# In a decoder kernel, the gathered key row's product reads h from PSUM, and a sample pair's scores pass through two PSUM banks

## The chip, the cores and the metric

The kernel runs on one core of a Trainium2 chip. The metric is the device time of one execution in microseconds (us); the time before is 2462.84 us, the median of three runs (2455.85 to 2471.47).

## What is computed

One step of a one-layer hybrid decoder for 528 prompt rows (512 tokens and 16 meta tokens) and 8 x 8 sample rows with a paged past of 2048 positions each. All data is float32. Three parts of the reference matter here. `peer` is the retrieval of single-neuron experts; `fox_sample` and `dsa_sample` are the two attentions of the sample rows over the past.

```python
def peer(x, ...):                       # x is h, the normalised rows
    ...                                 # 8 heads x top-16 experts for each token
    pre = jnp.einsum('thkd,td->thk', expert_u[experts], xb)      # key rows times h
    coef = (gate * jax.nn.gelu(pre, approximate=False)).astype(x.dtype)
    return jnp.einsum('thk,thkd->td', coef, expert_v[experts])   # value rows

def fox_sample(q, k, v, logf, cache_k, cache_v, cache_logf, page_table):
    ...
    p = jax.nn.softmax(jnp.concatenate([s_past, s_new], axis=-1), axis=-1)   # 2048 + 8 keys
    ...
```

## The kernel before

The kernel has three phases: the projection, the prompt's attention, and from about 440 us a third one in which five engines follow one written plan. The plan is a list of items; each engine goes through it in the same order and does its own part of every item. Its backbone is `gathers`: 1152 indirect DMAs issued by POOL (GpSimd, L918), each of 128 expert rows of 1024 floats (512 KB). 576 of them fetch key rows (`peer_u`, v = 0) and 576 value rows (`peer_v`, v = 1). They are for five token tiles i (four of 128 prompt tokens, one of 64 sample rows, whose experts are packed so that it needs only 64 key gathers). The order is: the 128 key gathers of tile 0, 72 value gathers of tile 0, and then the key gathers of the next tile woven with value gathers of earlier ones. The rows land in a ring of 10 slots (16 late in the phase); POOL waits for a slot's last reader before it issues into it.

- A key row is read by VectorE (`read_row`, L2081): row x h, summed over 1024 elements into one column of `pre`. h is `hrow[i]` (for the last tile `h_twice`), in SBUF as the row is. The operation is a custom one followed by the reading of its accumulator.
- A value row is read by TensorE (`add_rows`, L1369): four matmuls of 512 columns for one row, summed in PSUM banks 6 and 7. Its weights are strips written by ScalarE (L1699) from the coefficients, after GELU (L1596, `gelu`) and the product with the gate (L2053, `coefs`, VectorE).
- Between the gathers lie the other items: the merge and query products of tiles 1 to 3 (L1164, L1178, L1202), the routing (top-16 and selection on VectorE, `route`), and the sample's part.

The sample's part goes through eight pairs q (0 to 3 FoX, 4 to 7 DSA). For each q, TensorE makes the scores in five pieces c (`sample_scores`: four of 512 keys in banks 0 to 3, one of 8 in bank 4), VectorE takes the maximum over 2056 (`sample_max`, L1981), ScalarE the exponential from PSUM into `prob_s` in SBUF (`exponentials`, L1635) and the normalised weights in place (L1640); TensorE turns them in 16 transposes through banks 0 to 3 (`sample_turn`, L1302), ScalarE copies them out (L1648), and TensorE multiplies them with the values (`sample_weigh`, L1325), in bank 5. Before the pairs, the index scores use banks 0 to 3 by two and two (`index_products`, L1236, `index_relu`, L1604). SyncE (SP) issues the loads of weights and pages (`k_b`, `v_b`, `kv_a`, `kidx`) in an order of its own.

Which banks a stage holds sets what can be kept in PSUM:

```python
            at = gather_at[i, 0, 0]                     # first key gather of tile i
            out = bank(c)                               # scores of piece c, banks 0 to 3
            act.activation(prob_s, ps[:, 0:KEYS], ACT.Exp, bias=col(COL_SMAX), ...)
            dve.tensor_tensor_reduce(out=row, in0=row, in1=h, ..., accum_out=pre[:, k:k + 1])
```

## Time and profile before

| what | value |
|---|---|
| median of three runs | 2462.84 us (2455.85 to 2471.47) |
| span of the profiled execution | 2493.9 us |
| busy: PE, VectorE, POOL, ScalarE | 1810.2, 1433.9, 1307.8, 307.8 us |
| moved by DMA | 791.92 MB, of it 604.58 MB by POOL's queue |

The span of the profiled execution is 1.3% above the median of the timed runs; sums are made against the span and then scaled. PE is TensorE, DVE is VectorE, ACT is ScalarE, POOL is GpSimd, SP is SyncE. Busy time is summed over the whole span and says little about which engine ends a stage; the DMA columns of a table by stretches do: the share is the mean over 16 DMA engines of the time that their packets took, and can be slightly over 1 because packets overlap.

### The profile page before, as it was taken

The numbers are of one execution on the slowest core, as the hardware profiler recorded it, in microseconds if no ns is written. First come the engines' busy times: TensorE is split into PE (matmuls) and PEld (weight loads), VectorE is DVE, ScalarE is ACT, GpSimd is POOL, SyncE is SP. The second block draws the span as 40 slices with busy tenths as digits, with TensorE's granted clock in tenths as the row PEclk, the third lists the DMA queues.
The fourth block names the chain that finished last, engine by engine and source line by source line (L and its number), as shares of the span: only waits on it lengthen the run. The fifth ranks groups of instructions, "written<-read, shape, count | busy, mean of one in ns | idle before, by whom it ended". The sixth has DMA issues, their size and how long they took to land.

```text
span 2493.9 us, 23573 instructions
## 1 busy us (share of the span) xinstructions
PE 1810.2 (73%) x7244; PEld 768.0 (31%) x7247; DVE 1433.9 (57%) x3191; ACT 307.8 (12%) x732; POOL 1307.8 (52%) x1175
## 2 busy tenths in 40 slices
PE   9999988899699635566666766776777884555566
PEld 6767646644244201111112121221223250110011
DVE  2115876898845643999856569854444437434400
ACT  0214442111011101001101010110110010000000
POOL 1100000467655744555555557766777747677664
PEclk9998987999899867777778789998999997876678
DMA  5206322999989976999999999999999999999997
GB/s 182 71 3 195 102 85 68 355 328 410 361 306 368 346 281 238 394 367 400 386 401 380 401 371 362 371 356 368 378 384 409 409 370 374 364 359 380 355 377 287
DMA packets 259648, 791.92 MB, mean 318 GB/s; under 512 B 31522, under 2 KB 56163, under 8 KB 258947
## 3 DMA queue, kind: packets, MB, share of 16 engines
q0 software_dynamic: 166400, 604.58, 63.6%
q1 hardware_dynamic: 91268, 180.82, 20.6%
q10 hardware_dynamic: 1856, 5.03, 0.5%
q8 instruction: 58, 0.95, 0.2%
q14 instruction: 66, 0.54, 0.1%
HBM read 784.13 MB, written 5.59 MB: 317 GB/s over the span
## 4 chain that ended last, share of the span: by engine, by line
POOL 13%; DMA 10%; PE 8%; issue 7%; SPq 7%; another core or an unknown queue 6%; DVE 2%; ACT 1%; POOLq 0%
POOL arena L918 13%; DMA arena<-v_b 4%; PE ps L1369 3%; SPq L841 3%; DMA arena<-peer_v,arena 3%; SPq L768 2%; DMA arena<-peer_u,arena 2%; PE ps L1325 2%; DMA arena<-kv_a 2%; SPq L834 1%; PE ps L1202 1%; DVE arena L2081 1%; PE ps L1302 1%; ACT arena L1640 0%
## 5 line engine op out<-in xcount | busy, mean ns | idle before, releaser
L1369 PE MATMUL ps<-arena 128*32 128x512 f32 x2304 | 767.5, 717 | 346.6 <-DMA arena<-peer_v,arena 287.9
L2081 DVE CUSTOM_DVE_ANT_0 arena<-arena 128x1024 f32<-128x1024 f32 x576 | 694.7, 1225 | 531.5 <-DMA arena<-peer_u,arena 475.7
L918 POOL DMA_INDIRECT arena<-peer_v,arena x576 | 623.4, 1082 | 445.9 <-PE ps L1369 245.0
L918 POOL DMA_INDIRECT arena<-peer_u,arena x576 | 664.1, 1153 | 311.8 <-issue 162.2
L1369 PEld LDWEIGHTS ps<-arena 128*32 128x32 f32 x2304 | 153.4, 122 | 877.7 <-issue 662.1
L1164 PE MATMUL ps<-arena 128*128 128x448 f32 (+2 forms) x512 | 156.8, 467 | 13.1 <-DVE arena L1997 12.4
L1202 PE MATMUL ps<-arena 128*128 128x384 f32 (+2 forms) x704 | 146.5, 368 | 10.0 <-ACT arena L1576 8.1
L1325 PE MATMUL ps<-arena 128*64 128x512 f32 (+1 forms) x512 | 102.6, 538 | 68.1 <-DMA arena<-v_b 57.3
L900 POOL MEMSET arena<- 128x1024 f32 x1 | 1.0, 953 | 282.4 <-ACTq L723 282.4
L950 PE MATMUL ps<-arena 128*128 128x296 f32 (+1 forms) x512 | 132.1, 419 | 6.2 <-DMA arena<-xT 6.2
L1699 ACT ACTIVATE arena<-arena 128x8 f32<-128x8 f32 x72 | 15.3, 216 | 943.1 <-PE ps L1369 635.2
L1202 PEld LDWEIGHTS ps<-arena 128*128 128x128 f32 x704 | 104.3, 202 | 58.9 <-issue 26.8
L1164 PEld LDWEIGHTS ps<-arena 128*128 128x128 f32 x512 | 89.0, 193 | 87.0 <-issue 70.4
L950 PEld LDWEIGHTS ps<-arena 128*128 128x128 f32 (+1 forms) x512 | 96.9, 190 | 39.7 <-issue 8.3
L1284 PE MATMUL ps<-arena 128*32 128x512 f32 x256 | 51.6, 901 | 61.3 <-DMA arena<-k_b 61.0
L1325 PEld LDWEIGHTS ps<-arena 128*64 128x64 f32 x512 | 39.7, 159 | 144.0 <-issue 143.2
L895 POOL DMA_INDIRECT arena<-logf_b,arena x16 | 14.6, 913 | 126.4 <-PE ps L950 113.6
L2088 DVE SCALAR_TENSOR_TENSOR arena<-arena,ps 128x1024 f32<-128x1024 f32 (+1 forms) x5 | 6.1, 1219 | 126.2 <-PE ps L1369 84.6
L1967 DVE MAX8 arena<-arena 64x8 f32<-64x2056 f32 x32 | 73.6, 2299 | 1.0
L979 PE MATMUL ps<-arena 64*128 64x384 f32 (+9 forms) x168 | 69.9, 525 | 4.9 <-ACT arena L1545 1.9
L1968 DVE MATCH_REPLACE8 arena<-arena 64x2056 f32<-64x2056 f32 x32 | 73.1, 2286 | 0.0
L1825 DVE MAX8 arena<-arena 128x8 f32<-128x128 f32 (+3 forms) x120 | 34.2, 325 | 58.6 <-ACT arena L1583 53.2
(211 smaller groups left out, 1694.1 us busy)
## 6 DMA issues: line engine op xcount, KB each, us to landing
arena<-k_b SPq DMA_DIRECT2D x128, 256.0 KB
arena<-v_b SPq DMA_DIRECT2D x128, 256.0 KB
arena<-w_mix SPq DMA_DIRECT2D x56, 512.0 KB
arena<-w_q SPq DMA_DIRECT2D x48, 512.0 KB
arena<-kv_a SPq DMA_DIRECT2D x128, 128.0 KB
arena<-w_out SPq DMA_DIRECT2D x24, 512.0 KB
arena<-peer_u,arena POOLq DMA_INDIRECT x576
arena<-peer_v,arena POOLq DMA_INDIRECT x576
```

Of the source, the lines that this page charges most:

```text
L841: sp.dma_start(ring[s_][:, j * 256:(j + 1) * 256], io["kv_a"][bass.ds(nos[j], 1)].rearrange("o p n -> (o p) n")).then_inc(ring_loaded[s_], 16)
L918: pool.indirect_dma_start(out=rows[slot_of[n]], out_offset=None, in_=io["peer_v"] if v else io["peer_u"], in_offset=bass.IndirectOffsetOnA ...
L950: last = pe.matmul(bank(2 * (m % 2) + a, HT, 0, n), wring[m % 3][:, k, 0:n], xT[:, k, a * HT:(a + 1) * HT], start=(k == 0), stop=(k == KD ...
L979: last = pe.matmul(out, heads[0:rows_, q, q0:q0 + nq], heads[0:rows_, kt, c0:c1], start=True, stop=not biased)
L1164: last = pe.matmul(out, mw_k[u % NMW][:, k0 + k, :], src[:, k, :], start=(k == 0), stop=(k == nk - 1))
L1202: last = pe.matmul(bank(4 + n % 2, WIDTH[p]), mw_k[u % NMW][:, k, :], hT[p][:, k, :], start=(k == 0), stop=(k == KD - 1))
L1284: last = pe.matmul(out[32 * lane:32 * lane + 32], qs_flat[:, at + 32 * lane:at + 32 * lane + 32], kk[e][:, :, hp, :], start=(hp % 2 == 0), ...
L1325: last = pe.matmul(out[e], probT_s[:, c, j * 128 + 64 * e:j * 128 + 64 * e + 64], rhs, start=(c == 0 and j == 0), stop=False)
L1369: last = pe.matmul(bank(6 + a, 512, 32 * lane, 32 * lane + 32), strips[:, GT * (G % 2) + k % GT, MID - r_:MID - r_ + 32], rows[slot_of[n]] ...
L1967: step(dve.max(top8, isamp))
L1968: step(dve.match_replace(isamp, top8, isamp, TAKEN))
L2081: dve.tensor_tensor_reduce(out=row, in0=row, in1=h, scale=1.0, scalar=0.0, op0=ALU.mult, op1=ALU.add, accum_out=pre[:, k:k + 1]).then_inc( ...
```

## The change

- `read_row` reads h from PSUM. ScalarE copies h of tile i there once, before the tile's first key row (`place_h`, a new item `h_up`): tile 0 to banks 6 and 7, the others to banks 2 and 3. VectorE waits for the copy at the first key row of each tile; the copy waits until the key rows of the tile before have been read.
- To free banks 2 and 3 from the first key row of tile 1 on, the sample's part keeps to banks 0, 1, 4 and 5. The scores of a pair go alternately to banks 0 and 1, and a new item `s_keep` has ScalarE copy each piece into `prob_s`; the maximum and the exponential then read `prob_s`. The transposes alternate between banks 0 and 1, as do the key scores of tile 4 (`score_bank`); the index products have one pair of banks instead of two.
- The plan's positions don't move: each `s_score` with its `s_keep` takes the room that `s_score` had.

The diff, without the declaration of two semaphores and the two new branches of ScalarE's loop:

```diff
@@ -171,6 +171,10 @@
+        def h_bank(i):
+            return bank(2 if i else 6, D)
...
@@ -518,7 +523,8 @@
             out += [(("iy", 4), 2), (("admit",), 1)]
-            out += [(("s_score", 0, c), 5) for c in range(5)]
+            for c in range(5):
+                out += [(("s_score", 0, c), 1), (("s_keep", 0, c), 4)]
...
@@ -526,19 +532,22 @@
                     for c in range(5):
-                        out += [(("s_score", q + 1, c), 5), (("s_weigh", q, c), 5)]
+                        out += [(("s_score", q + 1, c), 1), (("s_keep", q + 1, c), 4), (("s_weigh", q, c), 5)]
                 else:
                     out += [(("s_weigh", q, c), g if c < 4 else 1) for c in range(5)]
                     out += [(("s_out", q), 36 if q == 3 else 16)]
                     if q + 1 < NB:
-                        out += [(("s_score", q + 1, c), 3) for c in range(5)]
+                        for c in range(5):
+                            out += [(("s_score", q + 1, c), 1), (("s_keep", q + 1, c), 2)]
                 if q + 1 < NB:
                     out += [(("s_max", q + 1), 2)] + ([(("s_out", q), 1)] if q < 3 else [])
                     out += [(("s_exp", q + 1), 2), (("s_norm", q + 1), 2), (("s_turn", q + 1), 3)]
             return out
+        for i in range(1, 5):
+            put(gather_at[i, 0, 0], "h_up", i)
         in_prompt = [("turn", 0), ("score", 0, 0)] + [("query", 0, m) for m in range(4)]
-        pre_items = [("routed0",)] + [item for item, _ in merge_items(0) if item not in in_prompt]
+        pre_items = [("h_up", 0), ("routed0",)] + [item for item, _ in merge_items(0) if item not in in_prompt]
...
@@ -563,6 +572,7 @@
         s_end = at
+        assert where["score", 3, 3] < where["h_up", 1]
...
@@ -642,7 +652,7 @@
             if kind == "s_score" and at[1] == 4:
-                return sx_done, at[0] + 1
+                return s_kept, 5 * at[0] + 5
...
@@ -708,6 +718,10 @@
             return qp_ready, 2 * PH * p + m + 1
+        def score_bank(i, g):
+            return g if i < 4 else g % 2
...
@@ -1208,11 +1222,13 @@
                 pe.wait_ge(qp_copied, 2 * PH * p + 4 * g + 4)
-                if i:
+                if p == 2 and g >= 2:
+                    pe.wait_ge(sc_copied, 4 * i + g - 1)
+                elif i:
                     pe.wait_ge(sc_copied, 4 * (i - 1) + g + 1)
-                for m in range(4 * g, 4 * g + 4):
-                    last = pe.matmul(ps[0:nt, m * 128:(m + 1) * 128], qpT[p][:, m, 128 * t:128 * t + nt], subk[:, m, :],
-                                     start=True, stop=True)
+                for m in range(4):
+                    last = pe.matmul(bank(score_bank(i, g), 512, 0, nt)[:, m * 128:(m + 1) * 128],
+                                     qpT[p][:, 4 * g + m, 128 * t:128 * t + nt], subk[:, 4 * g + m, :], start=True, stop=True)
...
@@ -1227,13 +1243,13 @@
                     pe.wait_ge(qp_copied, 4 * PH)
-                if c >= 2:
-                    pe.wait_ge(ix_read, 2 * (c - 1))
+                if c:
+                    pe.wait_ge(ix_read, 2 * c)
                 w = 512 if c < 4 else SN
                 keys = unit("ki", -1, c, 0).rearrange("p (a n) -> p a n", a=4) if c < 4 else kin
                 for g in range(2):
                     for p in (2 * g, 2 * g + 1):
-                        last = pe.matmul(bank(2 * (c % 2) + g, w), qis[:, p, :], keys[:, p, :], start=(p % 2 == 0),
+                        last = pe.matmul(bank(g, w), qis[:, p, :], keys[:, p, :], start=(p % 2 == 0),
...
@@ -1258,8 +1274,10 @@
                         pe.wait_ge(smask_ready, 1)
-                if q:
-                    pe.wait_ge(st_copied, 5 * (q - 1) + c + 1)
+                if q and c in (0, 1, 4):
+                    pe.wait_ge(st_copied, 5 * (q - 1) + (3, 4, 0, 0, 5)[c])
+                if c in (2, 3):
+                    pe.wait_ge(s_kept, 5 * q + c - 1)
...
@@ -1276,7 +1294,7 @@
                     return
-                out = bank(c)
+                out = bank(c % 2)
...
@@ -1291,15 +1309,17 @@
                                   start=True, stop=False)
-                pe.matmul(out, pick[:, pr, :], bias[:, c * 512:(c + 1) * 512], start=False, stop=True)
+                pe.matmul(out, pick[:, pr, :], bias[:, c * 512:(c + 1) * 512], start=False, stop=True).then_inc(ss_ready, 1)
             def sample_turn(q):
                 pe.wait_ge(sw_ready, q + 1)
                 for c in range(5):
                     if c < 4:
+                        if c >= 2:
+                            pe.wait_ge(st_copied, 5 * q + c - 1)
                         for j in range(4):
                             k0 = c * 512 + j * 128
-                            last = pe.transpose(ps[:, k0:k0 + 128], prob_s[:, k0:k0 + 128], ident)
+                            last = pe.transpose(bank(c % 2)[:, j * 128:(j + 1) * 128], prob_s[:, k0:k0 + 128], ident)
...
@@ -1580,7 +1600,7 @@
                     act.wait_ge(pair_routed, 4 * (i - 3) + 4)
-                act.activation(sc[SCB[i]][0:nt, 4 * g:4 * g + 4, :].rearrange("p a b -> p (a b)"), bank(g, 512, 0, nt),
+                act.activation(sc[SCB[i]][0:nt, 4 * g:4 * g + 4, :].rearrange("p a b -> p (a b)"), bank(score_bank(i, g), 512, 0, nt),
...
@@ -1601,7 +1621,7 @@
                         act.wait_ge(iy_ready, c)
-                    act.activation(relu_s[g][:, 0:w], bank(2 * (c % 2) + g, w), ACT.Relu).then_inc(ix_read, 1)
+                    act.activation(relu_s[g][:, 0:w], bank(g, w), ACT.Relu).then_inc(ix_read, 1)
...
@@ -1613,7 +1633,7 @@
                 else:
-                    act.wait_ge(ss_ready, q)
+                    act.wait_ge(ss_ready, 5 * q)
...
@@ -1628,11 +1648,26 @@
+            def place_h(i):
+                act.wait_ge(ln1_done, i + 1)
+                if i:
+                    act.wait_ge(dve_used, read_before[gather_at[i, 0, 0]])
+                if i == 4:
+                    act.wait_ge(h_packed, 16 * 2)
+                act.activation(h_bank(i), hrow[i] if i < 4 else h_twice, ACT.Copy).then_inc(h_placed, 1)
+            def keep_scores(q, c):
+                act.wait_ge(ss_ready, 5 * q + c + 1)
+                if q and c == 0:
+                    act.wait_ge(st_ready, 5 * q)
+                w = 512 if c < 4 else SN
+                act.activation(prob_s[:, c * 512:c * 512 + w], bank(c % 2 if c < 4 else 4, w), ACT.Copy).then_inc(s_kept, 1)
             def exponentials(q):
                 act.wait_ge(smax_ready, q + 1)
-                if q:
-                    act.wait_ge(st_ready, 5 * q)
-                act.activation(prob_s, ps[:, 0:KEYS], ACT.Exp, bias=col(COL_SMAX),
+                act.activation(prob_s, prob_s, ACT.Exp, bias=col(COL_SMAX),
...
@@ -1644,7 +1679,7 @@
                     act.wait_ge(st_ready, 5 * q + c + 1)
-                    dst, src = (probT_s[:, c, :], bank(c)) if c < 4 else (probTn, bank(4, 128, 0, SN))
+                    dst, src = (probT_s[:, c, :], bank(c % 2)) if c < 4 else (probTn, bank(4, 128, 0, SN))
...
@@ -1975,10 +2014,10 @@
             def sample_max(q):
-                dve.wait_ge(ss_ready, q + 1)
+                dve.wait_ge(s_kept, 5 * q + 5)
                 if q:
                     dve.wait_ge(sx_done, q)
-                dve.tensor_reduce(col(COL_SMAX), ps[:, 0:KEYS], AX_X, ALU.max, negate=True).then_inc(smax_ready, 1)
+                dve.tensor_reduce(col(COL_SMAX), prob_s, AX_X, ALU.max, negate=True).then_inc(smax_ready, 1)
...
@@ -2074,11 +2113,10 @@
                 row = rows[slot_of[n]]
-                h = hrow[i] if i < 4 else h_twice
-                if i == 4 and k == 0:
-                    dve.wait_ge(h_packed, 16 * 2)
+                if k == 0:
+                    dve.wait_ge(h_placed, i + 1)
                 dve.wait_ge(row_loaded[slot_of[n]], 16 * fill_of[n])
-                dve.tensor_tensor_reduce(out=row, in0=row, in1=h, scale=1.0, scalar=0.0, op0=ALU.mult, op1=ALU.add,
+                dve.tensor_tensor_reduce(out=row, in0=row, in1=h_bank(i), scale=1.0, scalar=0.0, op0=ALU.mult, op1=ALU.add,
                                          accum_out=pre[:, k:k + 1]).then_inc(dve_used, 1)
             def finish(i):
```

## Rows read from the trace of the kernel before

**Rows 1.** The page: the span, and the busy time of each engine.

```profile
span 2493.9 us, 23573 instructions
PE 1810.2 (73%) x7244; PEld 768.0 (31%) x7247; DVE 1433.9 (57%) x3191; ACT 307.8 (12%) x732; POOL 1307.8 (52%) x1175
```

**Rows 2.** Windows, third phase, two stretches: start:end, length, busy (count), granted clock, DMA.

```profile
core 0: us, PE busy (x) PEld busy (x) DVE busy (x) ACT busy (x) POOL busy (x), PEclk, DMA share, GB/s
1000.00:2050.00 1050.00, 738.05 (x2658) 227.89 (x2658) 686.56 (x1306) 111.01 (x241) 656.54 (x571) 0.86 1.00 383
2050.00:2475.00 425.00, 229.34 (x850) 50.71 (x852) 164.66 (x413) 12.99 (x39) 297.71 (x297) 0.75 0.97 367
```

**Rows 3.** Timeline of POOL: start, duration, line, form, count, idle time before.

```profile
1303.23 1.86 POOL L918 DMA_INDIRECT arena<-peer_v,arena  x1 [0.31 <-issue]
...
1308.75 0.94 POOL L918 DMA_INDIRECT arena<-peer_u,arena  x1 [0.30 <-issue]
```

**Rows 4.** Timeline of VectorE, the same stretch.

```profile
1303.06 1.23 DVE L2081 CUSTOM_DVE_ANT_0 arena<-arena 128x1024 f32<-128x1024 f32 x1 [2.18 <-DMA arena<-peer_u,arena]
...
1307.68 2.30 DVE L1967 MAX8 arena<-arena 64x8 f32<-64x2056 f32 x1
```

**Rows 5.** Groups of instructions: busy us, mean ns of one, idle time before, releaser.

```profile
L2081 DVE CUSTOM_DVE_ANT_0 arena<-arena 128x1024 f32<-128x1024 f32 x576 | 694.7, 1225 | 531.5 <-DMA arena<-peer_u,arena 475.7
L918 POOL DMA_INDIRECT arena<-peer_v,arena x576 | 623.4, 1082 | 445.9 <-PE ps L1369 245.0
L918 POOL DMA_INDIRECT arena<-peer_u,arena x576 | 664.1, 1153 | 311.8 <-issue 162.2
```

**Rows 6.** Groups by form, VectorE: 1024 elements with one input in PSUM, then none.

```profile
L2005 DVE SCALAR_TENSOR_TENSOR arena<-arena,ps 128x1024 f32<-128x1024 f32 x3 | 3.7, 1218 | 0.0
L1820 DVE SCALAR_TENSOR_TENSOR arena<-arena 128x1024 f32<-128x1024 f32 x4 | 5.1, 1285 | 0.1
```

**Rows 7.** Groups by form, ScalarE and the transposes.

```profile
L1302 PE MATMUL ps<-arena 128*128 128x128 f32 x128 | 22.2, 346 | 19.9 <-ACT arena L1640 19.9
L1648 ACT ACTIVATE arena<-ps 128x512 f32<-128x512 f32 x32 | 18.0, 601 | 16.4 <-PE ps L1302 9.6 <-remote 5.4 <-issue 1.4
L1569 ACT ACTIVATE arena<-ps 128x1024 f32<-128x1024 f32 x3 | 3.0, 1022 | 3.1 <-PE ps L1188 3.1
```

**Rows 8.** Windows of 50 us in the third phase, columns as in rows 2.

```profile
450.00:500.00 50.00, 45.02 (x172) 29.13 (x173) 46.91 (x133) 6.52 (x17) 23.67 (x19) 0.91 0.97 363
500.00:550.00 50.00, 45.09 (x119) 23.36 (x118) 48.95 (x126) 4.05 (x11) 32.45 (x24) 0.93 0.91 321
890.00:1000.00 110.00, 44.31 (x111) 12.81 (x111) 36.90 (x75) 6.89 (x15) 43.73 (x42) 0.69 0.69 241
1240.00:1290.00 50.00, 33.11 (x139) 9.10 (x139) 27.83 (x31) 0.22 (x1) 22.71 (x21) 0.73 1.04 399
1540.00:1590.00 50.00, 39.24 (x156) 11.31 (x155) 48.19 (x152) 10.35 (x17) 38.32 (x35) 1.00 0.96 350
1740.00:1790.00 50.00, 37.65 (x168) 12.49 (x169) 20.98 (x34) 10.56 (x25) 38.41 (x33) 0.97 0.94 350
1790.00:1840.00 50.00, 36.61 (x91) 7.46 (x90) 20.80 (x33) 7.31 (x8) 37.02 (x30) 0.86 1.03 401
2040.00:2090.00 50.00, 26.52 (x113) 8.14 (x111) 38.02 (x125) 1.70 (x6) 35.74 (x33) 0.73 0.93 331
2150.00:2200.00 50.00, 25.28 (x148) 5.71 (x144) 2.34 (x7) 2.46 (x6) 33.21 (x35) 0.84 0.98 372
2200.00:2250.00 50.00, 26.03 (x81) 4.95 (x73) 21.27 (x36) 0.76 (x4) 37.54 (x35) 0.67 0.96 359
2400.00:2450.00 50.00, 38.27 (x158) 10.82 (x154) 2.74 (x3) 1.09 (x5) 35.18 (x37) 0.92 0.99 378
```

**Rows 9.** Waits from 2050 to 2475 us: us in total, times, longest us.

```profile
POOL arena L918 <- issue: 83.5, 274, 0.3
POOL arena L918 <- remote: 33.4, 15, 4.1
```

**Rows 10.** Waits over the whole span: what ScalarE's GELU and its reader waited for.

```profile
ACT arena L1596 <- DVE arena L2081: 85.0, 6, 27.0
...
DVE arena L2053 <- ACT arena L1596: 45.9, 6, 20.6
```

**Rows 11.** Waits from 450 to 550 us.

```profile
POOL arena L918 <- DVE arena L2081: 34.4, 11, 12.3
```

More of the change, by code:

```diff
@@ L356, in program @@
         zero_s, spread_done, smask_ready = sem("zero_s"), sem("spread_done"), sem("smask_ready")
-        ss_ready, smax_ready, sx_done = sem("ss_ready"), sem("smax_ready"), sem("sx_done")
+        ss_ready, s_kept, smax_ready, sx_done = (sem(n) for n in ("ss_ready", "s_kept", "smax_ready", "sx_done"))
+        h_placed = sem("h_placed")
         sinv_ready, sw_ready, st_ready, st_copied = (sem(n) for n in ("sinv_ready", "sw_ready", "st_ready", "st_copied"))
@@ L1732, in _ @@
                     spread(*at)
+                elif kind == "s_keep":
+                    keep_scores(*at)
+                elif kind == "h_up":
+                    place_h(*at)
                 elif kind == "s_exp":
```

## The prediction

> **What bounds the kernel now.** I read the page's line of busy times first [rows 1]. TensorE leads with 73% of the span, but that average mixes stages, so I went to the table by stretches and to its DMA columns. From 1000 to 2050 us the 16 DMA engines are busy all the time at 383 GB/s, and from 2050 to 2475 us at a share of 0.97 and 367 GB/s [rows 2]. In the third phase the kernel is a stream of row gathers that runs at the speed of the DMA engines. What can be won there is time in which they are not full, and the question is who leaves them so.
>
> POOL is a candidate. A gather takes 0.94 us of POOL with 0.30 us before the next [rows 3], so POOL alone could issue one every 1.24 us. The mean is 1082 ns for value rows and 1153 ns for key rows [rows 5]: together 1287.5 us of busy time against 1152 x 0.94 = 1083 us, 205 us too much. The timelines show where it comes from. The gather that begins at 1303.23 us, inside a product that began at 1303.06 us and took 1.23 us, lasts 1.86 us: it ends at 1305.09 us, which is 0.80 us after the product's end. The gather of 1308.75 us begins inside a MAX8 of 2.30 us, which reads one input, and takes its plain 0.94 us [rows 3, 4]. So what holds POOL is a VectorE instruction with two inputs in SBUF, and 576 of these stand in the phase [rows 5].
>
> Whether that costs time is read stretch by stretch [rows 8]. From 1540 us POOL is busy 38.3 us, and with 35 x 0.30 us between gathers that makes 48.8 of 50 us: POOL has no slack, and DMA is at 350 GB/s. From 2150 us there are as many gathers with almost no product beside them (VectorE busy 2.3 us); POOL is busy 33.2 us, has 6 us of slack, and DMA is at 372. There POOL stands for up to 4.1 us at a time on something that no instruction of the program releases, 33.4 us in all from 2050 us on [rows 9]; I read it as the DMA queue being full. So the unhindered POOL is a little faster than the DMA engines, and the hindered one a little slower. The hindrance costs only the difference.
>
> **The product (`read_row`).** Its second input moves to PSUM. No row of before shows this custom operation so. The nearest are two fused operations of 1024 elements: 1218 ns with one input in PSUM, 1285 ns with both in SBUF [rows 6]. I take the difference, 67 ns, off each of the 576, 38.6 us of VectorE; the bounds are nothing, and 67 ns more in place of less. It is on the path only where VectorE is full: from 450 to 550 us it is busy 46.9 and 49.0 of 50 us with 43 gathers issued [rows 8], and POOL waits 34.4 us for it [rows 11]. 43 x 0.067 = 2.9 us. Elsewhere the product waits for its row, and the gain goes into that wait.
>
> The Trainium skill (Perfetto Trace Analysis, Optimizing Scalar/DVE Operations) speaks against the change: it gives VectorE's data access about 60 ns on SBUF and 125 ns on PSUM. By that the product would be about 65 ns longer, an estimate from the page, and the 2.9 us would be a loss of about the same size. The rows at hand point the other way, so the measurement decides here.
>
> **POOL no longer held.** With one SBUF input the product should be to POOL what MAX8 is. Of the 205 us only the DMA time lost counts. The stretches in which POOL was tight, or nearly, with products beside it are four [rows 8]. Where only gathers move, I take the mean of the two free stretches, 372 and 378, as full speed (375); where page loads are mixed in, the next stretch (401). 1540: 50 x (375 - 350) / 375 = 3.3 us. 1740: 50 x (401 - 350) / 401 = 6.4 us. 2040: 50 x (375 - 331) / 375 = 5.9 us. 2200: 50 x (375 - 359) / 375 = 2.1 us. Together 17.7 us. Bounds: nothing, if the queue was full anyway; and, if every stretch ran like the best, 1050 x (401 - 383) / 401 = 47.1 us and 425 x (378 - 367) / 378 = 12.4 us [rows 2, 8], 59.5 us. I choose the low side, since a gather issued sooner mostly waits longer in the queue.
>
> The Trainium skill (SBUF - State Buffer, Who interferes with whom) has the rule behind this: a VectorE instruction with two SBUF inputs contends with a GpSimd instruction that reads SBUF, one with at most one such input does not. This trace agrees with the first half (1.86 against 0.94 us); that the second half holds for an input in PSUM no row of before shows.
>
> **Copying h up (`h_up`).** Five copies of 1024 elements at about 1.02 us [rows 7], 5 us of ScalarE, which is busy 12% [rows 1]. The copy for tiles 2, 3 and 4 starts only when the last product of the tile before has read its row, and VectorE's next product waits for it: about 1.3 us each, four times at most. Behind VectorE then stand routing items and the freeing of slots; the ring of 10 or 16 rows covers that. Cost nothing, 5 us if the cover is gone.
>
> **Scores through two banks (`s_keep`).** ScalarE gets 32 copies of 512 columns at 601 ns [rows 7] and 8 small ones, some 21 us. Between two pieces the plan leaves 5 gathers (3 from pair 3 on), at 1.43 us or more each, so piece c + 2 comes 8.6 us or more behind piece c, and the copy of 0.6 us is long done. Only the last small copy, some 0.3 us with its wait, lengthens a pair's chain to the maximum, eight times. Maximum and exponential move to SBUF at about the same duration. ScalarE's queue now waits for TensorE five times in a pair instead of about once; behind it stand strips, which TensorE needs only eight rows later, and GELU, on which `coefs` waits. I cost it at nothing, covered by the gathers in flight.
>
> **Transposes and index scores.** 16 transposes took 16 x 346 ns = 5.5 us by their mean, 1.4 us for four; the third four now wait for a copy of 0.6 us that began when the first four ended [rows 7]. It is done before the second four are. At the full clock four may be shorter than a copy; then 0.5 us or so for a pair, eight times 4 us of TensorE, hidden by DMA. The index scores lose their second pair of banks where TensorE waits for page loads anyway (the stretch from 890 us, DMA at 241 GB/s [rows 8]); nothing. The key scores of tile 4 wait for two copies, about 1 us, far ahead of their use.
>
> **The sum.** 17.7 + 2.9 = 20.6 us off the span of 2493.9: 2473.3 us. The median of the runs is 0.9875 of the profiled span (2462.84 / 2493.9), so the forecast is 2442 us.
>
> **Rivals.** A, the forecast: 2442 us, by itself 2428 to 2453. Chance 0.42.
> B, POOL held back the whole phase: every stretch comes up to the best DMA rate. 59.5 + 2.9 = 62.4 us off, 2431.5 x 0.9875 = 2401 us. For it: 205 us too much of POOL, in both kinds of gathers [rows 5]. Against it: the share of 1.00 from 1000 us on leaves little room. Chance 0.21.
> C, the gain is swallowed: POOL's 205 us turn into waiting for slots or the full queue, or the product in PSUM holds POOL as before. 2463 us, 2453 to 2475. For it: [rows 9], and stretches with a blocked POOL at the full rate. Chance 0.24.
> D, slower: TensorE's piece c + 2 waits for ScalarE's copy of c, ScalarE stands behind a GELU that waits for VectorE (85.0 us in six waits, 27.0 at the longest [rows 10]), and the DMA queue runs dry. Such a stop of TensorE is seen from 890 to 1000 us: 110 x (1 - 241 / 399) = 44 us of DMA time lost, with 399 the full rate at 1240 us [rows 8]. One more of this size, and some 8 us of smaller ones, less nothing gained: 2494 + 52 = 2546, with A's 21 us taken off 2525 us, x 0.9875 = 2494 us. It decides from 46 us of new stops on (21 to undo the gain, 25 for 1%). Against it: the plan's distance of 6 to 20 gathers. Chance 0.13.
>
> **How the numbers follow.** A measurement of this kernel can tell about 1% (25 us) from no change; the bounds are 2438 and 2487 us. Below 2438 lie all of B and two fifths of A: 0.38. Above 2487 lies D: 0.13. Within: 0.49. The range from 2398 to 2480 us holds A, C and a good half of B, and leaves out D.
>
> **What would show it.** In the profile after: gathers of POOL at 0.94 us also inside a product, POOL's busy time near 1083 us for the 1152; the product near 1160 ns; stretches like that from 1540 us at 372 GB/s or more; POOL waiting longer for slots, TensorE or `remote`. Waits of the score matmuls for ScalarE's copies under 1 us each. Wrong would be: gathers of 1.6 to 2.0 us still there (C), DMA near 400 GB/s throughout (B), or a new wait of TensorE for `prob_s` copies above 10 us (D).

## The result: 3% slower

The kernel after took 2547.35 us, the one before 2467.15 us beside it on the same chip: ratio 1.031, 95% interval 1.023 to 1.038. (One timed run of 3059 us, at a granted clock of 0.54, is left out of the ratio as disturbed.) The forecast was 2442 us; the result lies outside its range, on the other side. The traces compared below show less than this loss: the profiled execution of before took 2493.9 us, at the upper end of its timed runs (2455.85 to 2494.95), and that of after 2547.7 us, so they differ by 53.8 us where the medians of the timed runs differ by 80.

The page of the kernel after, its span and busy times:

```profile
span 2547.7 us, 23627 instructions
PE 1796.3 (71%) x7244; PEld 769.6 (30%) x7247; DVE 1428.2 (56%) x3191; ACT 333.1 (13%) x777; POOL 1110.4 (44%) x1175
```

No engine but ScalarE, with its copies, works noticeably longer. POOL is busy 197 us less than in [rows 1], as the change was expected to bring, and the span is 53.8 us longer. The groups of instructions that answer to [rows 5] (busy us, mean ns, idle time before them and its releasers):

```profile
L2119 DVE CUSTOM_DVE_ANT_0 arena<-arena,ps 128x1024 f32<-128x1024 f32 x576 | 688.2, 1220 | 481.9 <-DMA arena<-peer_u,arena 348.3 <-issue 71.8 <-ACT ps L1658 49.4
L932 POOL DMA_INDIRECT arena<-peer_v,arena x576 | 545.1, 946 | 600.0 <-PE ps L1389 351.4 <-issue 148.7 <-remote 79.0
L932 POOL DMA_INDIRECT arena<-peer_u,arena x576 | 544.9, 946 | 408.0 <-DVE arena L2119 159.6 <-issue 149.8 <-PE ps L1389 80.1
```

Both kinds of gathers now take 946 ns by the mean, and one beside a product takes no longer. The two timelines of the same stretch, POOL and then VectorE (start, us, line, form, idle before):

```profile
1620.75 0.93 POOL L932 DMA_INDIRECT arena<-peer_v,arena  x1 [0.31 <-issue]
1621.99 0.94 POOL L932 DMA_INDIRECT arena<-peer_u,arena  x1 [0.30 <-issue]
```

```profile
1619.99 1.22 DVE L2119 CUSTOM_DVE_ANT_0 arena<-arena,ps 128x1024 f32<-128x1024 f32 x1
...
1621.13 1.22 DVE L2119 CUSTOM_DVE_ANT_0 arena<-arena,ps 128x1024 f32<-128x1024 f32 x1
```

The gather of 1620.75 us begins in one product and runs on into the next at its plain 0.93 us; in [rows 3] one that began so took 1.86 us. The time that POOL no longer loses beside products it now spends waiting, most of it for TensorE to free slots. Waits of POOL in the kernel after, then in before (us in total, times, longest):

```profile
POOL arena L932 <- PE ps L1389: 431.4, 95, 30.1
POOL arena L932 <- DVE arena L2119: 180.5, 98, 21.1
POOL arena L932 <- remote: 88.2, 41, 5.2
```

```profile
POOL arena L918 <- PE ps L1369: 293.6, 81, 25.9
POOL arena L918 <- DVE arena L2081: 90.1, 31, 12.3
POOL arena L918 <- remote: 50.3, 25, 4.1
```

And TensorE waits longer for two kinds of page loads. Its waits in the kernel after, then in before:

```profile
PE ps L1252 <- DMA arena<-kidx: 77.8, 4, 35.8
...
PE ps L1310 <- DMA arena<-kv_a: 51.4, 4, 16.5
```

```profile
PE ps L1236 <- DMA arena<-kidx: 54.6, 3, 30.3
PE ps L1292 <- DMA arena<-kv_a: 23.0, 3, 10.2
```

Together 129.2 against 77.6 us, 51.6 us more, about what the span has grown by. That the two agree proves nothing by itself: `banks_only` below, which loses nothing, waits 83.2 us for the same loads in its trace, and other runs below shed most of these waits and win hardly any time. The other page loads, k_b and v_b, are waited for 102 us after and 118 before.

Which stretch lost it is read by setting both traces side by side at the same gather, not at the same time. Gather 120 is issued 11 us earlier after than before, gather 144 9 us later, 288 23 us later, 576 24 later, 768 46, 840 52, and the last one 53. So nothing is lost or won between 300 and 600, nor from 840 on, where two of the four stretches lie in which the prediction had looked for its gain. The windows of equal work (gathers 293 to 600 and 600 to 840) in after, then in before; columns as in [rows 2]:

```profile
1040.00:1640.00 600.00, 381.15 (x1326) 102.44 (x1326) 469.35 (x890) 74.11 (x150) 289.58 (x305) 0.80 1.00 381
1640.00:2061.00 421.00, 289.59 (x1050) 97.98 (x1050) 182.80 (x331) 51.55 (x111) 227.24 (x242) 0.83 0.96 367
```

```profile
1015.00:1617.00 602.00, 391.45 (x1326) 106.15 (x1326) 475.97 (x912) 61.87 (x126) 354.46 (x309) 0.81 1.01 382
1617.00:2009.00 392.00, 297.08 (x1050) 94.06 (x1048) 180.71 (x317) 42.30 (x95) 276.46 (x240) 0.92 1.00 385
```

The first stretch has the same speed in both, 381 and 382 GB/s. The second, with the kv_a pages, has a DMA share of 0.96 where before had 1.00. TensorE is busy 69% of it (289.59 of 421 us) against 76% (297.08 of 392) in before, and its granted clock is 0.83 against 0.92.

Why are the pages late? The chain of the work that ended last goes through SyncE (SPq) where the kv_a loads begin. First the pieces of it in the kernel after (start, us, what); L782 is the line that brings page numbers into SyncE's registers, L855 issues the kv_a loads, "issue" is time with nothing waited for:

```profile
1620.83 1.68 SPq L782
...
1626.62 0.71 issue
1627.35 0.71 issue
1628.07 0.72 issue
1628.79 0.70 SPq L782
1629.49 0.70 issue
1630.21 0.72 SPq L782
1630.93 0.69 issue
1631.62 0.71 SPq L782
...
1635.26 0.33 SPq L855
```

In before the read of the next numbers and what follows it (L768 and L841 there) go by so:

```profile
1594.33 1.67 SPq L768
1598.21 0.33 SPq L841
1598.76 0.33 SPq L841
```

In the second chain 3.9 us lie between the start of the read and the first load, in the first 14.4 us (1620.83 to 1635.26): SyncE's register instructions advance one in about 0.70 us, either because one takes that long or after a pause of that length, where most take 0.15 us or less. Counted over the trace, 70 of them (50 us) took over 0.6 us before and 187 (133 us) after. They go with the gathers: of those at which no gather had been issued in the 10 us ahead (211 in after) none was that late, of those with eight in the 10 us 56% (64 of 114) in after and 29% (10 of 34) in before. And eight in 10 us, the pace of an unhindered POOL (1.24 us each), stood for 270 us of the time from 400 to 2060 us after and for 88 before. Pauses of this length come on top (48 us before, 98 us after); and from the start of a read of page numbers to the last test of them SyncE needs 286 us over all 80 reads before and 350 us after. That is an association within a trace; the runs below had to show what causes what.

### The profile page after: what moved, and what is told of

It reads as the page before. It is cut to its first block, busy times and chain, and to the rows that moved or that the text cites. A ratio compares the mean times of both kernels' runs of the same rounds, so it can differ in the third digit from the quotient of the medians.

```text
span 2547.7 us, 23627 instructions
## 1 busy us (share of the span) xinstructions
PE 1796.3 (71%) x7244; PEld 769.6 (30%) x7247; DVE 1428.2 (56%) x3191; ACT 333.1 (13%) x777; POOL 1110.4 (44%) x1175
## 2 busy tenths in 40 slices
DMA packets 259649, 791.92 MB, mean 311 GB/s; under 512 B 31523, under 2 KB 56164, under 8 KB 258948
## 4 chain that ended last, share of the span: by engine, by line
issue 11%; DMA 9%; another core or an unknown queue 9%; PE 9%; POOL 8%; SPq 8%; DVE 3%; ACT 1%; DVEq 0%; POOLq 0%; ACTq 0%
POOL arena L932 8%; PE ps L1389 4%; SPq L782 3%; DMA arena<-v_b 3%; SPq L855 3%; DMA arena<-peer_u,arena 2%; DMA arena<-k_b 2%; SPq L848 2%; DMA arena<-peer_v,arena 1%; PE ps L1345 1%; DVE arena L2119 1%; PE ps L1216 1%; PE ps L1192 1%; PE ps L1302 1%
## 5 line engine op out<-in xcount | busy, mean ns | idle before, releaser
L1389 PE MATMUL ps<-arena 128*32 128x512 f32 x2304 | 744.2, 725 | 324.5 <-DMA arena<-peer_v,arena 238.3
L2119 DVE CUSTOM_DVE_ANT_0 arena<-arena,ps 128x1024 f32<-128x1024 f32 x576 | 688.2, 1220 | 481.9 <-DMA arena<-peer_u,arena 348.3
L932 POOL DMA_INDIRECT arena<-peer_v,arena x576 | 545.1, 946 | 600.0 <-PE ps L1389 351.4
L932 POOL DMA_INDIRECT arena<-peer_u,arena x576 | 544.9, 946 | 408.0 <-DVE arena L2119 159.6
L1216 PEld LDWEIGHTS ps<-arena 128*128 128x128 f32 x704 | 106.0, 205 | 61.2 <-issue 28.4
L1178 PEld LDWEIGHTS ps<-arena 128*128 128x128 f32 x512 | 92.6, 203 | 87.8 <-issue 71.5
L1302 PE MATMUL ps<-arena 128*32 128x512 f32 x256 | 52.0, 876 | 68.6 <-DMA arena<-k_b 55.2
L1192 PE MATMUL ps<-arena 128*128 128x512 f32 (+1 forms) x128 | 64.7, 649 | 20.5 <-DVE arena L2036 9.0
L1252 PE MATMUL ps<-arena 128*128 128x512 f32 (+1 forms) x40 | 24.2, 765 | 77.8 <-DMA arena<-kidx 77.8
L1666 ACT ACTIVATE arena<-ps 128x512 f32<-128x512 f32 (+1 forms) x40 | 20.3, 514 | 409.7 <-PE ps L1312 312.7
```

The source lines that it names most:

```text
L932: pool.indirect_dma_start(out=rows[slot_of[n]], out_offset=None, in_=io["peer_v"] if v else io["peer_u"], in_offset=bass.IndirectOffsetOnA ...
L1178: last = pe.matmul(out, mw_k[u % NMW][:, k0 + k, :], src[:, k, :], start=(k == 0), stop=(k == nk - 1))
L1192: last = pe.matmul(bank(2 * t + a, 512, 0, nt), hT[p][:, k, 128 * t:128 * t + nt], mw[u % NMW][:, a * 512:(a + 1) * 512], start=(k == 0), ...
L1216: last = pe.matmul(bank(4 + n % 2, WIDTH[p]), mw_k[u % NMW][:, k, :], hT[p][:, k, :], start=(k == 0), stop=(k == KD - 1))
L1302: last = pe.matmul(out[32 * lane:32 * lane + 32], qs_flat[:, at + 32 * lane:at + 32 * lane + 32], kk[e][:, :, hp, :], start=(hp % 2 == 0), ...
L1389: last = pe.matmul(bank(6 + a, 512, 32 * lane, 32 * lane + 32), strips[:, GT * (G % 2) + k % GT, MID - r_:MID - r_ + 32], rows[slot_of[n]] ...
```

## Experiments

Ratios are to the kernel before, run beside each, with 95% intervals.

**The operand or the banks?** `banks_only` is the kernel after with h read from SBUF; four others read it from PSUM in some tiles only.

```diff
-in1=h_bank(i), scale
+in1=hrow[i] if i < 4 else h_twice, scale                                # banks_only
+in1=h_bank(i) if i == 0 else hrow[i] if i < 4 else h_twice, scale      # psum_tile0
+in1=h_bank(i) if i else hrow[i], scale                                  # psum_tiles1to4
+in1=h_bank(i) if i == 3 else hrow[i] if i < 4 else h_twice, scale      # psum_tile3
+in1=h_bank(i) if i in (2, 4) else hrow[i] if i < 4 else h_twice, scale # psum_tiles2_4
```

> The changed kernel, but the product reads h from SBUF as before; the copies of h into PSUM, their waits and the two banks of the sample's part stay. Theory 'crowding' (the unhindered gathers take DMA time from the page and weight loads, TensorE gets its pages later and its slots stop POOL): the gathers are hindered again, POOL's mean goes back to 1.08 to 1.15 us, and the time is that of before within 0.5% (2455 to 2480 us). Theory 'banks' (the two banks, the copies of the scores by ScalarE and the wait for the copy of h cost the time): the loss stays, 2535 to 2560 us. Half and half would be near 2505 us.

> The changed kernel with h in PSUM for tile 0 alone; tiles 1 to 4 read h from SBUF. In the comparison of the two traces the changed kernel is 9 us behind at gather 144, after it was 11 us ahead at gather 120. Crowding: this stage alone is unhindered, so it keeps about those 9 us and nothing of what comes later: 2472 to 2485 us. Banks: as the changed kernel, 2535 to 2560 us.

> The changed kernel with h in PSUM for tiles 1 to 4, tile 0 from SBUF. Crowding: the stages of the sample's pages and the last merge are lost as in the changed kernel (44 us of its 53), the merge of tiles 1 to 3 is not: 2505 to 2540 us. Banks: 2535 to 2560 us.

> The changed kernel with h in PSUM for tile 3 alone (gathers 632 to 884, beside the sample's DSA pairs with their kv_a pages of 1 KB a partition, and the last merge). In the traces the kernel with tiles 1 to 4 in PSUM loses 10 us at the index keys (gathers 240 to 264), some 5 in the FoX pairs, 17 to 20 us from gather 600 to 850 and nothing behind. Crowding of small packets: 15 to 25 us over the kernel before here too, ratio 1.005 to 1.012. A disturbance by the reads from PSUM, spread evenly over the products: 128 of 448 of the 2.5%, ratio 1.00 to 1.007 with the loss spread over all the tile's gathers.

> The changed kernel with h in PSUM for tiles 2 and 4 alone (the FoX pairs with pages of 2 KB a partition, and the end with gathers alone). Crowding: no loss to speak of, ratio 0.99 to 1.005, POOL's gathers unhindered in 40% of the products. Even disturbance: 192 of 448 of 2.5%, ratio 1.005 to 1.015.

Measured: `banks_only` 0.993 (0.987 to 0.999), `psum_tile0` 1.006 (1.001 to 1.011), `psum_tiles1to4` 1.025 (1.017 to 1.034), `psum_tile3` 1.006 (1.003 to 1.010), `psum_tiles2_4` 1.005 (1.000 to 1.010). Two banks, the copies of the scores and of h cost nothing that can be measured; all the loss comes with the product's operand. The first three came as the theory of crowding expected. The last two don't decide: 1.006 fits both of the theories put down for `psum_tile3`, and 1.005 for `psum_tiles2_4` lies on the border between them. In `banks_only` POOL is held as in before:

```profile
L932 POOL DMA_INDIRECT arena<-peer_u,arena x576 | 664.6, 1154 | 336.1 <-issue 161.4 <-DVE arena L2119 95.8 <-PE ps L1389 62.3
L932 POOL DMA_INDIRECT arena<-peer_v,arena x576 | 610.5, 1060 | 438.6 <-PE ps L1389 230.6 <-issue 150.5 <-remote 45.5
```

Against `banks_only` tile 0 costs 1.3% and tiles 1 to 4 3.2%, together more than the 3.8% of all five: the price is spread over the tiles and roughly adds up, no single place makes it.

**A slower POOL.** `pool_delayed` gives POOL a small write of 0.12 us to wait for after each gather.

```diff
                                         ).then_inc(row_loaded[slot_of[n]], 16)
+                pool.memset(idle[:], 0.0).then_inc(idled, 1)
+                pool.wait_ge(idled, n + 1)
```

> The changed kernel, and POOL clears 8 columns of a small tile and waits for that after each gather, a few tenths of a us, about as much as the products held it back before (0.18 us a gather). Crowding by the mean pace of POOL: most of the loss comes back, 2465 to 2500 us. Banks: no gain, 2540 us or more. If crowding is right but it was the moments of the hindrance and not the mean pace that mattered, it also stays at 2540 us while the kernel with the product from SBUF is at 2470 us.

Measured: 1.021 (1.013 to 1.029), between the two outcomes expected and so a miss for both. A part comes back (TensorE's wait for kv_a is 40.5 us, the late register instructions 121), though the end of the kernel, where only gathers run, pays for the delay (some 12 us more than after needs from gather 888 on).

**Crowding of the page loads themselves?** Both kernels with page loads of a quarter of their partitions; the rest of the pages is left out, so the samples' scores are not the reference's.

```diff
...
-sp.dma_start(ring[s_][:, j * 256:(j + 1) * 256],
-             io["kv_a"][bass.ds(nos[j], 1)].rearrange("o p n -> (o p) n")
+sp.dma_start(ring[s_][0:32, j * 256:(j + 1) * 256],
+             io["kv_a"][bass.ds(nos[j], 1), 0:32].rearrange("o p n -> (o p) n")
...
```

The edit does the same to the loads of k_b, v_b and kidx.

> The kernel before, loading only a quarter of each page of the sample's caches (the index keys, k_b, v_b, kv_a): the first 32 partitions (16 of 64 for the index keys) instead of all, so the sample's attention is computed from what else lies in the ring. It is the baseline for the next one. The pages are some 143 MB of 792; without three quarters of them the DMA engines carry 107 MB less, at 383 GB/s 280 us less if DMA is the bound: 2190 to 2300 us.

> The changed kernel with the same quarter of the pages loaded, the rest of each page left out. Crowding (page loads against unhindered gathers): with a quarter of the load there is little to crowd out, so the loss of 3.1% shrinks to under 1% against the kernel before with quarter loads, or turns into a gain from the faster POOL (0.98 to 1.01 of it). If instead reading h from PSUM disturbs TensorE or ScalarE at their PSUM accesses, the loss stays at 2.5 to 4% of it, since the same products run.

Measured: 0.973 (0.963 to 0.984) and 0.996 (0.991 to 1.000). After is still 2.3% above before when three quarters of the page bytes are gone. The size of the loads is not what makes them late. Both runs missed what was expected of them: under 1% of loss was expected by crowding, and 2.3% lies close to the 2.5 to 4% of the rival, a disturbance of TensorE or ScalarE by the reads from PSUM, which only the next runs rule out. That before gained only 2.7% says something on the bound too. The expectation took the pages for 143 MB; by the pages of the profile 66 MB are gone (725.86 of 791.92 MB left), which at 383 GB/s would be 172 us, an estimate, and 68 us came off. So the DMA engines, busy as they are, don't set the pace alone. In the trace of before with quarter loads TensorE still waits 45.2 us for kidx.

**Fewer gathers under way.** Now the suspicion of the chain above: gathers that come back to back. A wait lets gather n go only when gather n - K has landed.

```diff
+                if n >= K:
+                    pool.wait_ge(row_loaded[slot_of[n - K]], 16 * fill_of[n - K])
                 pool.indirect_dma_start(out=rows[slot_of[n]], out_offset=None,
```

> The kernel after, with one wait more on GpSimd: gather n is issued only when gather n-5 has landed, so that at most five of the 512 KB gathers are under way. Nothing else changes, the products still read h from PSUM and hold GpSimd up no longer. Theory 'bursts': with GpSimd free the gathers are issued back to back until the DMA queues are full (pairs under 1.35 us apart: 64% of the gathers before, 83% after), and what else comes over the DMA engines, instructions of the other engines' programs among it, arrives late (SyncE's register instructions that take over 0.6 us: 70 with 50 us in the trace of before, 187 with 133 us after, none of them where no gather was issued in the 10 us ahead, over half of them where eight were). It expects the slow register instructions to fall below 110 and the time to fall by 20 to 60 us against after's 2547, to 2490 to 2525. Theory 'operand': the products' reads of PSUM themselves cost the other engines the time; it expects no gain, 2540 to 2560.

> The kernel after with at most seven gathers under way, between the five that gave back all of the loss (2490) and none (2547). Theory 'bursts' makes it a matter of dose: between the two, 2495 to 2535, ratio 1.005 to 1.025, with 70 to 150 slow register instructions. Were it the wait instruction or its place that helped, and not the length of the queue, it would equal the run with five: 0.997 to 1.005.

> As the run with five, with at most three gathers under way (1.5 MB). Theory 'bursts': if a gather lands within some 4 us of its issue this is still at the pace of the DMA engines (512 KB in 1.24 us) and the queues are shorter still, so slow register instructions below 70 and 2450 to 2510 us; if a gather needs longer than 4 us the limit itself holds the gathers up and the time rises above 2560, with idle time of GpSimd at waits for a DMA. Theory 'operand': 2540 or more in either case.

> The kernel before with the same limit of five gathers under way. It is the control: does the limit help a kernel whose GpSimd is already held up by the products? Theory 'bursts' expects less gain than in after, since the queues are full less often: 0 to 25 us off before, 0.990 to 1.000. Theory 'operand' expects no change either, within 1%. A rise by over 1% would say that the limit has a price of its own, to be taken off the reading of the runs of after.

> The change's banks, copies and orders, the product's operand in SBUF again, and at most five gathers under way: the fourth corner of operand by limit. Known: banks 0.993, after 1.031, after with the limit 1.002, before with the limit 1.003. Theory 'bursts': with the queue kept short the operand's place is worth next to nothing, so this run is within 1% of after_flight5: 0.993 to 1.007. Theory 'operand has a price of its own besides the bursts': this run stays below after_flight5 by more than 1.5%, under 0.987.

Measured, in this order: 1.002 (0.997 to 1.007), 1.030 (1.023 to 1.037), 1.194 (1.184 to 1.203), 1.003 (0.999 to 1.008), 1.012 (1.005 to 1.020). Five under way give all of the 3.1% back, with h still in PSUM and POOL still unheld (945 and 947 ns a gather). TensorE's waits in `after_flight5`:

```profile
PE ps L1254 <- DMA arena<-kidx: 50.9, 2, 30.8
PE ps L1312 <- DMA arena<-kv_a: 17.6, 3, 9.4
```

68.5 us against 129.2, with 55 late register instructions against 187. POOL now spends its freedom on the new wait and much less on slots:

```profile
POOL arena L934 <- PE ps L1391: 213.9, 70, 24.0
POOL arena L934 <- DMA arena<-peer_u,arena: 141.6, 130, 3.3
...
POOL arena L934 <- DMA arena<-peer_v,arena: 101.1, 97, 2.9
```

It isn't the wait instruction that helps: seven under way have the same instruction and give nothing back (157 late register instructions, 131.6 us for kidx and kv_a). The middle value that was expected did not come: the loss acts as a step between five and seven. The signs between are less abrupt: POOL waits 86.8 us for landings with seven and 242.7 us with five, and eight gathers in 10 us stood for 177 us with seven, for 61 us with five and for 270 us without a limit. Why the time steps all the same isn't known. Three under way are too few: a gather lands 5.2 us after the start of its issue by the median (4.2 us at the least), no register instruction is late, and POOL waits over 1,000 us for landings:

```profile
POOL arena L934 <- DMA arena<-peer_v,arena: 540.1, 340, 4.9
POOL arena L934 <- DMA arena<-peer_u,arena: 532.9, 319, 5.8
```

`before_flight5` and `banks_flight5` show that the operand in PSUM has no price of its own: with five under way the SBUF versions aren't faster than `after_flight5`. (`banks_flight5` came out above its range of 0.993 to 1.007; why it is the slowest of the three is open, and four runs are few.) They show also that fewer late instructions aren't always time won. `before_flight5` has only 7, TensorE waits 5.5 us for kv_a and kidx together, and the time stays: POOL waits 186 us for landings, and the lead it has over before at gather 336 (30 us) is down to 10 us at the end.

**Bursts in the kernel before.** Up to gather 790 POOL waits at each fourth gather for four free slots.

```diff
-                prior = last_in[n]
-                if prior is not None:
+                for m_ in range(n, min(n + 4, SWITCH, len(gathers))) if n % 4 == 0 and n < SWITCH else [n]:
+                    prior = last_in[m_]
+                    if prior is not None:
...
```

> The kernel before with its gathers made to come in bursts: up to gather 790 GpSimd waits at every fourth gather until the slots of four are free and issues them in a row. Products, banks and copies are those of before. Theory 'bursts' (crowding by gathers that come back to back): more slow register instructions than the 70 of before, over 110, and a rise by 15 to 60 us, 1.006 to 1.025. Theory 'operand': the burst alone does nothing that matters, since a burst of four still leaves six of the ten slots filled ahead of the reader: 0.995 to 1.005.

Measured: 1.016 (1.007 to 1.024), inside the number expected, but not for its reason. The late register instructions fell to 47, and TensorE waited 25.1 us for kidx and kv_a. The waits for slots grew instead, for VectorE from 90.1 us to

```profile
POOL arena L919 <- DVE arena L2082: 204.4, 53, 14.3
```

Gathers were held back and came late. Nor did the edit make the bursts that it was meant to make: eight gathers in 10 us stood for 60 us, in before for 88. So the run says nothing for or against their effect.

**Through SyncE, or through every queue?** The page numbers are written into the program, so that SyncE has no register instructions for them; other pages than the reference's are read.

```diff
-                return nc.values_load_multi_w_load_instructions(
-                    pages[0:1, at:at + n], engines=(mybir.EngineType.SP,), min_val=0, max_val=NPOOL - 1)[1]
+                return [(37 * (at + j) + 11) % NPOOL for j in range(n)]
```

> The kernel before with the page numbers written into the program, (37*(place)+11) modulo the size of the pool, in place of being read out of SBUF by SyncE: the same number of page loads of the same size, from other pages, so that the scores and sums of the samples are of other pages than the reference's; SyncE's 80 reads of page numbers and the register instructions around them (320 us of SyncE's time in the trace of before) are gone. It is the control for fixed_pages_after. SyncE is then ready with the loads earlier in the index keys (890 to 1015 us) and the last stage of scores; expected 2400 to 2475.

> The kernel after with the same fixed page numbers (same part changed: other pages are read). Theory 'late issue': the bursts hurt mainly through SyncE, whose register instructions come late, so that the page loads are issued late and TensorE waits for kidx (76 us against 51 us with five in flight) and kv_a (51 us against 18 us). Without those instructions the ratio of this kernel to fixed_pages_before falls from 1.031 to 1.000 to 1.015. Theory 'all queues': every transfer and every engine's instructions come late behind a full queue of gathers, SyncE's only as one of them; the ratio of the two stays at 1.020 to 1.035.

Measured: 0.996 (0.992 to 1.000) and 1.004 (1.000 to 1.008). The loss of after against its control is 0.8% (2469.24 / 2450.87) in place of 3.1%. POOL is as free as in after, the bursts are there (eight gathers in 10 us for 238 us), and TensorE waits for kidx no more and for kv_a no longer than the control (18.0 us):

```profile
L931 POOL DMA_INDIRECT arena<-peer_u,arena x576 | 545.1, 946 | 423.2 <-DVE arena L2118 189.7 <-issue 154.0 <-PE ps L1388 68.9
```

```profile
PE ps L1309 <- DMA arena<-kv_a: 19.1, 3, 8.8
```

So about three quarters of the loss go through SyncE's late instructions (the intervals allow from about half to nearly all); the bursts alone, with nothing of this kind to delay, cost little. The control tells also what TensorE's waits are worth: in before 59.6 of the 77.6 us for kidx and kv_a went away with the numbers, and the time fell by 0.4%.

**Fewer such instructions.** The test that each page number lies in the pool is left out; the numbers are read and used as before.

```diff
-pages[0:1, at:at + n], engines=(mybir.EngineType.SP,), min_val=0, max_val=NPOOL - 1)[1]
+pages[0:1, at:at + n], engines=(mybir.EngineType.SP,), min_val=0, max_val=NPOOL - 1,
+    skip_runtime_bounds_check_because="the page tables hold numbers of the pool's pages only")[1]
```

> The kernel before without the bounds test that SyncE makes of every page number (two of its register instructions for each of the 512 numbers): the same page numbers are read and the same pages loaded. SyncE issues the page loads of each ring slot earlier. Fixed pages, which take all register instructions of the numbers away, gave 0.9957; with the tests alone gone it expects 0.993 to 1.000.

> The kernel after without the same tests. With the numbers fixed the loss against its own control fell from 3.1% to 0.8%. Theory 'late issue' (the bursts delay the instructions of SyncE's program, each at a time, and with them the page loads): fewer instructions are fewer to be late, so about half of the loss is gone, 1.008 to 1.022 of before. Theory 'the reads of the numbers out of SBUF are what is late' (the 80 reads stay): the loss stays, 1.024 to 1.034.

Measured: 0.992 (0.988 to 0.996) and 1.006 (1.003 to 1.009). The two stand 1.6% apart (2492.83 / 2453.2): about half of the loss is gone, as the theory of late instructions had it, though 1.006 lies just under its range, which began at 1.008 of before. Half as many register instructions are left (1026 of 2050), and 88 are late against 187, the same 9% of them. TensorE's waits in `unchecked_after` are down from 129.2 us to 57.3 (30.6 in `unchecked_before`):

```profile
PE ps L1253 <- DMA arena<-kidx: 38.1, 2, 23.0
...
PE ps L1311 <- DMA arena<-kv_a: 19.2, 3, 9.9
```

`unchecked_before`, 0.8% under before, is the fastest kernel with the whole computation; `banks_only` is level with it within the intervals.

## Why the prediction was wrong

- **POOL's hold: right.** 1152 gathers at 0.94 us were to be busy 1083 us; they are 1090 us. The second half of the rule that the Trainium skill gives (SBUF - State Buffer, Who interferes with whom), that a VectorE instruction with at most one SBUF input leaves GpSimd alone, holds here for a product with its other input in PSUM: 0.93 us for the gather shown beside one, 946 ns by the mean.
- **The product's 67 ns: mis-sized.** It became 1220 ns from 1225 ns. The difference between two other operations [rows 6] did not carry over to this one; the 2.9 us shrink to 0.2. The 65 ns more, the estimate from the Trainium skill (Perfetto Trace Analysis, Optimizing Scalar/DVE Operations), did not come either.
- **The copies, banks and transposes: right in sum.** `banks_only` is not slower. Rival D's mechanism did not happen: the waits of TensorE in after show none of the score matmuls for ScalarE's copies of the scores and 1.4 us in all for those of the transposes, and the wait of 41.6 us for the last `h_up` stands in place of one of 40.5 us for the row in before. VectorE waited 7.8 us for one other `h_up`, not about 1.3.
- **The 17.7 us of POOL no longer held: the step that failed.** Two faults lie in it. The gain isn't there: from gather 293 to 600 both kernels run at 381 and 382 GB/s, and from gather 864 to the last before needs 413 us and after 415 us. A stretch of 350 GB/s was read as one that POOL limits, but POOL's freed time (197 us busy less) went into waits: 138 us more for TensorE and 90 us more for VectorE to free slots, 38 us more for `remote`, as rival C had it. The premise under it, that the third phase runs at the speed of the DMA engines, is shaken too: a twelfth of the bytes left out brought 68 us where that speed says 172. And the bound was wrong: "nothing, if the queue was full anyway" excluded a loss. The sentence "a gather issued sooner mostly waits longer in the queue" was not followed to its end: it was not asked who shares the DMA engines with that queue, or which engine's instructions stall beside it. POOL's hold had kept the stretches with eight gathers in 10 us at 88 us; without it they stood for 270 us, SyncE's late register instructions went from 70 to 187, and a gain of 17.7 us became a loss of 53.8 us of span, which is gone with five gathers under way and down to 0.8% of the time with fixed page numbers.
- **Rival D's number, 2494, and its chance.** Its side was right; its time was not, with 2547 us measured. Its 52 us of new stops, before A's gain came off, are near the 53.8 us between the traces by luck, since the mechanism is one that no rival named. The profile of before held the hint: the chain of waits there goes 2% through L768, with SyncE's steps of 0.69 and 0.70 us near 1608 and 1618 us, and the waits for kidx and kv_a, 77.6 us, stood in its trace.

**What stays open.** Why a register instruction takes 0.70 us while gathers come back to back. The Trainium skill (Runtime: NRT & Kernel Launch, Instruction fetch mechanics) calls the cost of fetching the next block of instructions mostly hidden. A fetch for each late instruction is excluded by the page of after: the two queues of kind "instruction" moved 125 packets in the whole span, and 187 instructions of SyncE alone were late (queue, packets, MB, share):

```profile
q8 instruction: 58, 0.95, 0.2%
q14 instruction: 67, 0.54, 0.1%
```

What does delay the step no run tells. Open too are the step between five and seven gathers under way, and the last 0.8%, which is there with fixed page numbers.

## What to carry to other kernels

Before freeing an engine that issues transfers, ask what its slowness kept short: a faster issuer sends its transfers closer together, and an engine that issues small, timely transfers with instructions of its own can pay for it. Compare traces at equal work, gather by gather, and follow the late transfer back to its issue before blaming its bytes. If the issuer has become too fast, a wait on the landing of the transfer K before is a cheap brake, but K has to be found: here 5 was right, 7 did nothing and 3 cost 19%. And a wait that a change takes away is not yet time won: `before_flight5` took 72 us of TensorE's waits for pages away and was no faster.

## What the hardware showed that was not expected

- SyncE's register instructions, most of them 0.15 us or less, often took about 0.70 us during runs of gathers 1.24 us apart: none of 211 with no gather in the 10 us ahead, 64 of 114 with eight.
- The price of one operand in PSUM for a VectorE product of 1024 elements was nothing that shows (1220 against 1225 ns), and it took the whole hold off GpSimd (946 against 1082 and 1153 ns).
- At most five gathers of 512 KB under way were enough for the kernel's pace, three were not (317 and 267 GB/s over the span, 311 without a limit).
